# Two transformer blocks on one core: weighted sums of the modulation ahead of the weighing, half a gate projection under branch B's norms, other PSUM banks for the embedded rows

## What is computed

```python
mod_l = split(silu(c) @ ada_w[i] + ada_b[i], 6)        # shift, scale, gate, twice; the same with c_ctx
h = rms_norm(x) * (1 + mod_l[1]) + mod_l[0]
x = x + mod_l[2] * mixer(h)                            # layer 0: retention with 4 heads; layer 1: differential attention
x = x + mod_l[5] * swiglu(modulate(x, mod_l[3], mod_l[4]), ffn_w_in[i], ffn_w_out[i])
```

```python
q, k, v of branch A (8 heads), of branch B (12 heads in 3 groups), gl = split(x @ w_in)
h = (sigmoid(ga) * (oa @ w_branch_a) + sigmoid(gb) * (ob @ w_branch_b)) @ w_out
x = layer_norm(a * x + h)
ple = sigmoid(x @ w_ple_gate + b) * (p[i] @ w_ple)     # the embedded rows
x = layer_norm(a * x + relu(x @ w_up) ** 2 @ w_down + ple)
```

## Time and profile before

| what | value |
|---|---|
| median of 3 runs | 2157.18 us (2155.42 to 2157.25) |
| the profiled execution | 2155.47 us, its span 2153.7 us |
| PE busy | 2020.6 us, 94% of the span |
| DVE, ACT, POOL busy | 1331.9, 849.6, 68.4 us |
| DMA, share of 16 engines | q1 (weights) 37.9%, q0 (POOL's) 7.7% |
| granted clock of TensorE, mean | 0.977 |

### The profile page before, as it was taken

One profiled execution on the slowest core, in us unless ns is written; L12 is line 12 of the kernel. 1 busy time (PEld: TensorE's weight loads), 2 busy tenths in 40 slices (PEclk: granted clock), 3 DMA queues, 4 the chain that ended last, 5 costly groups with the idle time before them and its releaser, 6 DMA issues.

```text
span 2153.7 us, 27084 instructions
## 1 busy us (share of the span) xinstructions
PE 2020.6 (94%) x11090; PEld 1714.2 (80%) x11090; DVE 1331.9 (62%) x1640; ACT 849.6 (39%) x993; POOL 68.4 (3%) x121
## 2 busy tenths in 40 slices
PE   5898989898999999989888999999999999999998
PEld 3677777777888887767667998888799988888997
DVE  3866868556566556375666445666775566667555
ACT  5323313123322222145565443464444445545442
POOL 0000000000011001000000000000000000000000
PEclk9999999999999999999998999999999999999999
DMA  9543434233355444232224664554465545437552
GB/s 333 169 137 101 137 118 137 98 127 109 98 160 157 122 127 146 93 98 78 79 62 135 177 195 138 200 179 154 159 215 193 180 160 181 161 131 231 188 187 78
DMA packets 250733, 319.28 MB, mean 148 GB/s; under 512 B 10097, under 2 KB 166034, under 8 KB 250098
## 3 DMA queue, kind: packets, MB, share of 16 engines
q1 hardware_dynamic: 234880, 262.24, 37.9%
q0 software_dynamic: 14416, 53.14, 7.7%
q10 hardware_dynamic: 1314, 2.18, 0.3%
HBM read 316.47 MB, written 1.05 MB: 147 GB/s over the span
## 4 chain that ended last, share of the span: by engine, by line
PE 76%; DVE 12%; DVEq 4%; ACT 3%; ACTq 2%; issue 2%; DMA 1%; SPq 0%
PE ps L2175 23%; PE ps L2176 23%; PE ps L2177 23%; PE ps L2192 4%; DVE w_lo L1226 4%; DVE raw L1341 2%; ACTq L604 1%; DVEq L1336 1%; ACT w_hi L595 1%; DMA raw<-ret_w_in 1%; PE ps L2348 1%; DVEq L1243 1%; ACT arena L847 1%; DVE st L1655 1%; DVE hT_lo L1231 1%
## 5 line engine op out<-in xcount | busy, mean ns | idle before, releaser
L1226 DVE TENSOR_TENSOR w_lo<-raw,w_hi 128x2048 fp32r<-128x2048 f32 (+1 forms) x244 | 553.0, 2272 | 357.1 <-ACT w_hi L595 356.0
L595 ACT ACTIVATE w_hi<-raw 128x2048 fp32r<-128x2048 f32 (+1 forms) x244 | 461.7, 1896 | 262.1 <-PE ps L2177 246.3
L2175 PE MATMUL ps<-h_hi,w_hi 128*128 128x256 f32 x1120 | 320.5, 286 | 2.9 <-DVE h_lo L1231 2.9
L2176 PE MATMUL ps<-h_lo,w_hi 128*128 128x256 f32 x1120 | 318.4, 284 | 0.0
L2177 PE MATMUL ps<-h_hi,w_lo 128*128 128x256 f32 x1120 | 318.3, 284 | 0.0
L2175 PE MATMUL ps<-w_hi,big_hi 128*128 128x512 f32 x760 | 299.7, 394 | 14.9 <-DVE mod L1323 6.1
L2176 PE MATMUL ps<-w_lo,big_hi 128*128 128x512 f32 x760 | 296.5, 390 | 0.0
L2177 PE MATMUL ps<-w_hi,big_lo 128*128 128x512 f32 x760 | 296.4, 390 | 0.0
L2175 PEld LDWEIGHTS ps<-h_hi,w_hi 128*128 128x128 f32 x1120 | 216.3, 193 | 5.5 <-issue 4.4
L2176 PEld LDWEIGHTS ps<-h_lo,w_hi 128*128 128x128 f32 x1120 | 216.4, 193 | 0.8 <-issue 0.2
L2177 PEld LDWEIGHTS ps<-h_hi,w_lo 128*128 128x128 f32 x1120 | 216.2, 193 | 0.0
(11 more groups left out here) (289 smaller groups left out, 2649.9 us busy)
## 6 DMA issues: line engine op xcount, KB each, us to landing
raw<-ffn_w_in SPq DMA_DIRECT2D x88, 512.0 KB, 5.1
raw<-w_in SPq DMA_DIRECT2D x80, 512.0 KB, 4.6
raw<-w_up SPq DMA_DIRECT2D x64, 512.0 KB, 4.8
raw<-w_down SPq DMA_DIRECT2D x64, 512.0 KB, 4.5
raw<-ret_w_in SPq DMA_DIRECT2D x48, 512.0 KB, 4.7
front<-ada_w POOLq DMA_DIRECT2D x24, 1024.0 KB, 5.5
raw<-ffn_w_out SPq DMA_DIRECT2D x40, 512.0 KB, 4.4
raw<-ada_w POOLq DMA_DIRECT2D x64, 256.0 KB, 3.1
```

The source lines that it names most:

```text
L595: act.activation(SPLIT_HI[PAIR_OF[u]][:, 0:m], raw[:, RAW_OF[u], 0:m], ACT.Copy).then_inc(sem["hi_ready"], 1)
L1226: op(SPLIT_LO[PAIR_OF[u]][:, 0:m], raw[:, RAW_OF[u], 0:m], SPLIT_HI[PAIR_OF[u]][:, 0:m].bitcast(F32), ALU.subtract).then_inc(sem["lo_ready ...
L2175: pe.matmul(out, a[0], b[0], start=start, stop=False)
L2176: pe.matmul(out, a[0], b[1], start=False, stop=False)
```

## The change

Five edits.

1. In the heads, DVE runs `mod_sums(b)` ahead of the split of va, and `mod_sums(b + 2)` and the fourth piece ahead of the split of vb; only the last `mod_sums(b)` stays behind it.
2. In the feed-forward of layer 0 the last chunk but one is turned after u20 rather than u18, the last one inside strip e2, after its first k-step, and not after u21. Ten of the 16 last pieces are weighed by the end of the u-chunks, three after the split of `ahead("e0")` and three after that of `ahead("e1")`.
3. At the start of each layer of the second half, `x_lo` of the first tile comes after one split unit and not two.
4. In branch B, PE runs the first half of gate 5 ahead of the first `p_turned_b`, and DVE copies the first half of the turned probabilities ahead of the split of a unit (`ahead("G3")`).
5. The embedded rows go to banks 2 to 5 and not 0 to 3; the wait for banks 0 and 1 moves behind them. `branch_b` and `mix_lo` run in pairs.

```diff
@@ DVE, heads
                 i.then_inc(sem["roped"], 1)
-                ahead(f"g0{h}")
                 if h:
                     mod_sums(b)
+                ahead(f"g0{h}")
+                weigh()
+                mod_sums(b + 2)
                 weigh()
                 ahead(f"g1{h}")
-                weigh()
-                mod_sums(b + 2)
                 mod_sums(b)
                 ahead(f"va{h}")
@@ DVE, feed-forward of layer 0
                 up(i)
-                if i in (15, 18, 21):
+                if i in (15, 20):
                     mod_sums(4 if i % 2 else 6)
-                if i < 21:
-                    weigh(2 if i % 3 == 2 else 3)
+                if i < 19:
+                    weigh(2)
+            weigh(2)
             ahead("e0")
+            weigh(3)
             ahead("e1")
+            weigh(3)
+            mod_sums(0)
             used("e2")
@@ PE, the same place (the loop's extra at 15, 20 as above)
-            used(strip(4, "e2", hid, 19, 3, range(3), False, True))
+            strip(4, "e2", hid, 19, 3, (0,), False, False)
             pe.wait_ge(sem["gm_ready"], 22)
+            extra(0)
+            used(strip(4, "e2", hid, 19, 3, (1, 2), False, True))
+            mod_read()
             used(strip(0, "e3", hid, 11, 4, range(4), True, False))
@@ DVE, start of layer(l)
+                split(base + 1)
+                x_lo(0, 6)
                 split(base + 2)
-                x_lo(0, 6)
@@ DVE, branch B
+                pt_half_b(0)
                 ahead("G3")
-                pt_half_b(0)
                 pt_half_b(1)
@@ DVE, mixing
-                branch_b(0)
-                for i in range(1, 4):
+                for i in (0, 2):
                     branch_b(i)
-                    mix_lo(i - 1)
-                mix_lo(3)
+                    branch_b(i + 1)
+                    mix_lo(i)
+                    mix_lo(i + 1)
@@ PE, branch B (gate(g, r, js) runs the halves js of a gate)
                 gate(4, 14)
+                gate(5, 15, (0,))
                 p_turned_b(0)
                 s_read(3)
                 scores_b(1)
                 pt_read(3)
                 p_turned_b(1)
-                gate(5, 15)
+                gate(5, 15, (1,))
@@ PE, embedded rows
-                pe.wait_ge(p_read[0], ring(l, 20))
-                pe.wait_ge(p_read[1], ring(l, 21))
-                            i = product(bank(2 * t + c), xs, ...)
+                            i = product(bank(2 + 2 * t + c), xs, ...)
                 embedded(0).then_inc(sem["ple_full"], 1)
                 used(embedded(1))
                 w = unit("BB", 0, 2)
-                pe.wait_ge(sem["ple_read"], 2 * l + 1)
                 pv_read(4)
+                pe.wait_ge(p_read[0], ring(l, 20))
+                pe.wait_ge(p_read[1], ring(l, 21))
```

More of the change, by code:

```diff
@@ L1163, in layer @@
                 act.wait_ge(sem["ple_full"], s.next("ple_full"))
-                act.activation(PLE[:, 0, :], bank(0, 2), ACT.Copy, scale=0.5).then_inc(sem["ple_read"], 1)
+                act.activation(PLE[:, 0, :], bank(2, 2), ACT.Copy, scale=0.5).then_inc(sem["ple_read"], 1)
                 used("PL")
-                act.activation(PLE[:, 1, :], bank(2, 2), ACT.Copy, scale=0.5).then_inc(sem["ple_read"], 1)
+                act.activation(PLE[:, 1, :], bank(4, 2), ACT.Copy, scale=0.5).then_inc(sem["ple_read"], 1)
                 ahead("PL")
@@ L2838, in values_b, with gate @@
                     i.then_inc(sem["pv_full"], 1)
-                def gate(g, r):
-                    ring_free(r)
+                def gate(g, r, js=(0, 1)):
+                    if js[0] == 0:
+                        ring_free(r)
                     w = unit(f"G{g}", 0, KD)
-                    for j in range(2):
+                    for j in js:
                         i = chunk(bank(r % 2)[:, j * 256:(j + 1) * 256], w, j, h2, KD)
-                    used(i)
+                    if js[-1] == 1:
+                        used(i)
                 def branch_a(n, half, r):
@@ L2945, in embedded @@
                             xs = [v[:, PIN0 + k * 256 + t * P:PIN0 + k * 256 + (t + 1) * P] for v in (big_hi, big_lo)]
-                            i = product(bank(2 * t + c), xs, [v[:, k, c * 512:(c + 1) * 512] for v in w], k == 0, k == 1)
+                            i = product(bank(2 + 2 * t + c), xs, [v[:, k, c * 512:(c + 1) * 512] for v in w], k == 0, k == 1)
                     return i
```

## The result

| what | before | after |
|---|---|---|
| median | 2156.3 us, 4 runs (2154.47 to 2157.25) | 2117.34 us, 4 runs (2116.62 to 2119.23) |
| profiled execution, its span | 2155.47, 2153.7 us | 2119.23, 2117.4 us |
| granted clock, mean | 0.977 | 0.984 |

The ratio is 0.9822, 95% interval 0.9805 to 0.9839: faster by 1.8%. The profiled execution is the slowest of the four, 1.9 us above the median.

What follows compares the result with a forecast made beforehand. With PE busy 94% of the span, its remaining idle time was what could be won: 31.0 - 4.7 - 0.9 + 2 x (2.2 + 1.15 + 0.15) = 32.4 us, profiled 2155.5 to 2123.1, median 2125 us, range 2115 to 2134.

Steps and rivals of the forecast that it cites:

- Edit 1, 31.0 forecast: Four heads: DVE's new order turns queries and keys 7.75 us earlier in each, 31.0 us won (28.4 to 33.6).
- the second short wait of 0.3 us: Head 1: after the third k-step PE waits 0.3 us for the last `mod_sums(b)`, then turns at 199.65.
- rival (b): Heads: the fourth piece stays behind ACT's work for g1, so only 15 us are won, time 2141; chance 0.09.
- Edit 2, 4.7 lost forecast: Strips: PE waits 9.4 us in e2 instead of 6.1 ahead of e0, 4.7 us lost (3 to 6.5).
- e0, e1 and the first k-step of e2 are 108 matmuls: Strips: these take 24.5 us from e0's start at 856.5 to 881.0, when PE needs the last piece.
- win nothing, as PE did not wait there: Feed-forward of layer 0: weighing fewer pieces among the u-chunks gains no time.
- Rival (a)'s extreme: Strip e2: no wait left at all, e2 ending at 886.5 and the time 2112.5 us; chance 0.08.
- The row behind this price: Trace row of a third piece, started 4.8 us after POOL's issue; 4.3 us taken for the last piece.
- Edit 3, 0.75 won and 1.65 lost forecast: Second half's layer starts: 0.75 us won in layer 0, 1.65 lost in layer 1, together 0.9 lost.
- The bound of 2 us: Both layer starts: upper end of the 0 to 2 us loss, if a longer wait costs clock too.
- Edit 4, 2.2 a layer forecast: Branch B: 3.3 us won, then 1.4 us waited ahead of the third `p_turned_b`: 2.2 a layer (1.5 to 3.3).
- Edit 5, 1.3 a layer forecast: Embedded rows and mixing: 1.15 us a layer from the banks, 0.15 (0 to 1.2) from the pairs.

Runs made afterwards that it cites:

- the kernel with the pieces early: After, with late pieces weighed among the u-chunks again, last chunk but one turned after u18, two splits ahead of layer 1's `x_lo`: 2101.77 us.

## Why the prediction came out right, and 7.7 us high

The waits came and went as the forecast said, in every stage; what it lacked is the clock behind short waits in the second half, where luck helped it. By the spans 36.3 us went, and 32.4 were forecast. The other 3.8 of the 7.7 are not the kernel: the profiled execution of after stood 1.9 above its median, where the forecast had added 1.7 because before's stood that much below, and the rest is rounding.

**Edit 1, 31.0 forecast.** 32.2 by the timelines, 31.0 by the medians of the kernel with this edit alone. Head by head it is 7.9, 8.65, 7.3 and 8.4 (the shifts of the turned values), and I had 8.4 for head 1, 7.1 for head 2 and 7.75 for the others; the second short wait of 0.3 us did not come: PE turns queries and keys at the moment when the third k-step ends. Short waits of 1 us do leave the clock alone here, as assumed (1.00 in the windows behind all four). One reading was the wrong way round: against rival (b) the prediction says that ACT's high part was there 1.2 us before DVE's split of va. In the kernel before DVE was ready at 179.04 and stood idle for 1.21 us until ACT had it at 180.2; the sum's new place fills that hole.

**Edit 2, 4.7 lost forecast.** 3.8 by the timelines, 3.2 by medians. The wait was foreseen at 9.4 and is 9.30; the last piece was foreseen to start 4.3 us behind POOL's issue and does so after 4.26. The term that failed is "e0, e1 and the first k-step of e2 are 108 matmuls" set against e0's old start: the chunk that is turned in e2 is no longer turned ahead of e0, and I had charged its eight transposes, 0.8 us, twice. What the prediction says of fewer pieces among the u-chunks, that they "win nothing, as PE did not wait there", was right, and I should have gone on: then the pieces need not have moved at all. Rival (a)'s extreme, no wait in e2, is what the kernel with the pieces early reaches: it was named there as a case of luck, the pieces coming in time, and is a matter of order.

The row behind this price held, 4.26 us against 4.3. An estimate by the rule of the Trainium skill's page "DMA: Bandwidth & Descriptors" (Anatomy of one DMA) has the piece come 2.6 us after the issue; the trace does not agree where SP's load is under way, and the measurement decides.

**Edit 3, 0.75 won and 1.65 lost forecast.** 0.75 won, 1.55 lost. The two waits at layer 1's start are 1.84 and 1.11 us as worked out. In three other kernels with the same waits the clock fell behind them, in after it didn't, and that was luck. From these waits to the one ahead of O2 163.8 us pass in after and 166.6 in two of the three, 2.8 more; in the third, with the copy behind the split, 166.0, of which some 0.5 are the copy's. With 1.7 to 2.8 us lost as well, the two starts would have lost 2.5 to 3.6 us. The bound of 2 us, meant to hold this case, was too narrow.

**Edit 4, 2.2 a layer forecast.** 2.36 in layer 0. PE waits 0.91 us ahead of the third `p_turned_b` and not 1.4. In layer 1 it is 4.3: there the kernel before ran at 0.90 of the clock behind the two waits, and the kernel after at 1.00. That is 1.5 us (21.20 us from 1861.07 to 1882.27, where the same stretch of layer 0 takes 19.66); another 0.3 are a shorter wait ahead of the third `p_turned_b`, 0.58 us. The term was missing: the prediction took its rows from layer 0, where the same two waits had left the clock alone, and counted them twice. As another kernel kept its clock in layer 1 behind these waits (the last section), the 1.5 us are in part luck.

**Edit 5, 1.3 a layer forecast.** 1.6. The banks gave 1.37 where 1.15 stood, the pairs 0.3 where 0.15 stood.

The terms sum up: 1.2 (heads) + 0.9 (strips) + 0.1 (edit 3) + 2.2 (branch B, both layers) + 0.6 (edit 5), less 1.15 in stages that no edit touches (PE lost 0.75 us between the heads and the strips and 0.4 behind them), is 3.9 us. The 0.75 are clock too: behind a wait of 4.5 us that both kernels have, it was 0.56 over 7 us in after and 0.66 in before, and PE came to its next wait there after 18.86 us and not 18.15.

## What to carry to other kernels

Look at what a stalled engine's supplier was itself waiting for: here DVE stood idle ahead of a split while ready work, for which PE was waiting, lay behind it in its list, and moving that work forward was worth the wait and a third as much again in clock. Price a moved block at both ends: the weighing in the strips was taken from a place where it cost nothing and put behind a chain of split, fetch and piece, and leaving it where it was is worth 11.7 us there. And where the profile names the last of several releasers, put only the next one back before believing that it is the cause.

## What the runs showed of the hardware

**Whether a short wait costs clock is not settled by its length.** The waits of 7.2 us in the heads were always followed by half the clock; waits of 0.8 to 1.15 us there never were; waits of 2.2 us there were followed by a slow stretch each (0.67 over 5.2 us in head 1). But the pair of 1.04 and 2.13 us in branch B left the clock alone in layer 0 and brought it down in layer 1, the same instructions. The two rows of the first fence below are windows of the kernel before in layer 0 and in layer 1. In the kernel with the banks alone layer 1 kept its clock behind the same waits (second fence).

```profile
1467.00:1480.00 13.00, 12.64 (x113) 12.08 (x114) 10.86 (x19) 8.23 (x14) 0.12 (x1) 1.00 0.74 240
...
1861.00:1881.00 20.00, 17.80 (x150) 16.80 (x151) 16.02 (x24) 10.45 (x21) 1.58 (x3) 0.91 0.56 184
```

```profile
1861.00:1881.00 20.00, 17.81 (x163) 16.80 (x164) 16.63 (x24) 10.53 (x22) 1.59 (x3) 1.00 0.53 186
```

That is 1.5 us for the same instructions (19.66 us, 1861.06 to 1880.72, against 21.20, 1861.07 to 1882.27). The pair of 1.84 and 1.11 us at layer 1's start did it in the three other kernels that have it (with edits 3 to 5 alone 0.60, with the last pieces ahead of e3's split 0.62, with the copy behind its split 0.80 over the 8.4 us from the end of the first wait on) and not in after. Executions of one and the same kernel differ too: of the 13 of before, the four with a mean granted clock of 0.976 took 2156.7 to 2157.31 us, the eight with 0.978 took 2153.83 to 2156.14 (one, with 0.977, took 2156.91). What decides it, these runs do not tell: it stays open. The Trainium skill's page "TensorE: Matmul & The Clock Gate" (Part 1) says that the chip's watch on TensorE's activity runs freely, so that the same kernel varies with its phase. This would fit executions that differ only in when they come to the place, and no run here tests it. In a forecast, a pair of waits of 1 to 2 us needs a term for it: where the clock fell here, that cost 1.5 to 2.8 us.

**A fetch from POOL beside SP's load.** Issued 1.8 us after SP had begun to issue for 1 MB, a fetch of 256 KB took 4.26 us to DVE's start in the kernel after (SP from 850.47, POOL at 852.31) and 4.77 in the kernel before (SP from 567.82, POOL at 569.66). Issued 2.6 us after SP had begun with 0.75 MB, it took 3.11 (841.42 to 844.53). The median landing of such fetches, in the page of after, is 3.3 us. That SP's load is the cause is inferred from these three places; no run separates the two transfers.

```profile
raw<-ada_w POOLq DMA_DIRECT2D x64, 256.0 KB, 3.3
```
